# Output projection of a two-layer hybrid block: six of eight block pairs by seven products, the gated terms added to x in DRAM

## What is computed

```python
D_MODEL = 2048
D_FF = 4 * D_MODEL
...
    # gated merge of the D_MODEL-wide branch projections, then one output projection
    br = jnp.stack([o_att, o_fnet, o_ssm.astype(o_att.dtype), o_gmlp], axis=2)  # (b,L,4,MIX_W)
    gates = jax.nn.sigmoid(gate_logits.reshape(b, L, N_BRANCH, D_MODEL))
    merged = jnp.sum(gates * jnp.einsum('blkw,kwd->blkd', br, w_branch), axis=2)
    x = x + g1 * (merged @ w_out)
    # channel mixer: squared-ReLU MLP
    h2 = _rms(x) * (1 + sc2) + sh2
    x = x + g2 * (jnp.square(jax.nn.relu(h2 @ w_ff1)) @ w_ff2)
```

## Time and profile before

| | us |
|---|---|
| three timed runs | 4756.03, 4796.99, 5115.18 |
| median | 4796.99 |
| the profiled execution | 4768.78 |
| its span on the slowest core (core 1) | 4767.3 |
| spans of the eight cores | 4731.1 to 4767.3 |
| PE busy | 4562.7 (96% of the span) |
| DVE, ACT, POOL busy | 2463.3, 1910.8, 914.6 |
| output projection in the span, layer 0 and layer 1 | from 1336.6 and from 3633.6, some 137 each |

### The profile page before, as it was taken

The page is one execution under the profiler, slowest core; times in us unless marked ns, Lnnn a source line. Parts: engine busy times, 40 slices in busy tenths (PEclk is TensorE's granted clock), DMA queues, the critical chain, the costliest instruction groups (busy, mean ns, idle before and its releaser), DMA issues.

```text
span 4767.3 us, 90058 instructions; the slowest of 8 cores (4731.1 to 4767.3 us)
## 1 busy us (share of the span) xinstructions
PE 4562.7 (96%) x31548; PEld 2878.4 (60%) x31548; DVE 2463.3 (52%) x5081; ACT 1910.8 (40%) x4031; POOL 914.6 (19%) x1362
## 2 busy tenths in 40 slices
PE   3989898999999999999999998999999999999999
PEld 1445455566655777777755544655666567777776
DVE  4266645565546444444564575555654644444343
ACT  2134523333225444353544453333322453535352
POOL 1122110000101232424112201000010014141404
PEclk9979999999999999999999999999999999999999
DMA  8862755446776797979778446334578459494949
GB/s 192 136 118 65 170 99 99 80 85 128 131 198 122 120 152 121 152 118 154 159 191 150 92 109 124 67 63 79 109 136 196 100 95 148 76 151 74 153 72 128
DMA packets 266571, 585.63 MB, mean 123 GB/s; under 512 B 43792, under 2 KB 137488, under 8 KB 265872
## 3 DMA queue, kind: packets, MB, share of 16 engines
q0 software_dynamic: 171072, 441.53, 57.4%
q1 hardware_dynamic: 95056, 138.34, 9.1%
HBM read 818.05 MB, written 129.76 MB: 199 GB/s over the span
## 4 chain that ended last, share of the span: by engine, by line
PE 89%; DMA 6%; issue 2%; DVE 2%; ACT 1%; POOL 0%; SPq 0%; DVEq 0%; ACTq 0%; POOLq 0%
PE psum L1837 38%; PE psum L692 20%; PE psum L1651 18%; PE psum L1616 5%; DMA arena<-wm 2%; PE psum L1092 1%; DMA mgs<-arena 1%; PE psum L833 1%; PE psum L1074 1%; DMA arena<-wg 1%; PE psum L1133 1%; ACT arena L743 1%; DMA arena<-lc 1%; PE psum L1094 1%; DVE arena L754 1%
## 5 line engine op out<-in xcount | busy, mean ns | idle before, releaser
L1837 PE MATMUL psum<-arena 128*128 128x320 f16 x13216 | 1802.8, 299 | 0.0
L1837 PEld LDWEIGHTS psum<-arena 128*128 128x128 f16 x13216 | 1289.5, 98 | 508.7 <-issue 10.1
L754 DVE TENSOR_TENSOR arena<-arena 128x1024 f16<-128x1024 f16 (+9 forms) x2178 | 1080.6, 519 | 662.6 <-PE psum L1837 334.9
L743 ACT ACTIVATE arena<-arena 128x320 f16<-128x320 f32 (+8 forms) x1687 | 825.3, 508 | 870.1 <-DVE arena L754 528.3
L692 PE MATMUL psum<-arena 128*128 128x512 f16 (+2 forms) x5680 | 1092.0, 352 | 16.7 <-DVE arena L758 8.4
L1651 PE MATMUL psum<-arena 128*128 128x320 f16 x6720 | 1009.3, 300 | 14.7 <-ACT arena L743 6.0
L692 PEld LDWEIGHTS psum<-arena 128*128 128x128 f16 x5680 | 556.1, 99 | 504.1 <-issue 98.8
L754 DVE TENSOR_TENSOR arena<-psum,arena 128x320 f32<-128x320 f32 (+5 forms) x1110 | 539.2, 490 | 617.5 <-PE psum L1651 239.9
L1651 PEld LDWEIGHTS psum<-arena 128*128 128x128 f16 x6720 | 637.5, 98 | 330.9 <-issue 92.4
L743 ACT ACTIVATE arena<-psum,arena 128x320 f32<-128x320 f32 (+3 forms) x904 | 487.1, 554 | 664.7 <-PE psum L1837 531.8
L769 ACT COPY arena<-psum 128x320 f32<-128x320 f32 (+6 forms) x683 | 293.5, 440 | 581.8 <-PE psum L1837 259.4
(11 more groups left out here) (107 smaller groups left out, 1455.5 us busy)
## 6 DMA issues: line engine op xcount, KB each, us to landing
arena<-w POOLq DMA_DIRECT2D x256, 512.0 KB, 7.0
arena<-wm POOLq DMA_DIRECT2D x192, 512.0 KB, 7.4
arena<-wg POOLq DMA_DIRECT2D x128, 512.0 KB, 6.2
y<-arena POOLq DMA_DIRECT2D x256, 160.0 KB, 7.3
xs<-arena POOLq DMA_DIRECT2D x192, 160.0 KB, 8.2
arena<-xin SPq DMA_DIRECT2D x32, 640.0 KB, 23.5
arena<-xs SPq DMA_DIRECT2D x32, 640.0 KB, 14.9
arena<-dftA SPq DMA_DIRECT2D x32, 512.0 KB, 4.4
```

The lines of the kernel that those rows point to most:

```text
L743: return e.activation(out=lz(o), in_=lz(i), func=func, scale=scale, **kw)
L754: lambda e: e.tensor_tensor(out=lz(o), in0=lz(a), in1=lz(b), op=op), r=r, w=w, prio=S.p - boost, tag=tag)
L1837: ins = e.matmul(ps.ap()[:, 0:SUBS], lhsT=wv(kc), rhs=rhs(kc), start=first and kc == 0, stop=kc == 7, skip_group_check=True)
```

## The change

- Pairs (5,13), (4,12), (3,11), (2,10), (1,9), (0,8) of the output projection go through `sunits` with their own weight sums (`wsums`, which writes one of the four sums over a weight block, leaving one buffer of `SL` for the squares). Blocks 6, 14, 15 and 7 stay dense, as one group of four, last.
- The input sums of `M` (`tsums`) are made at the end of the gates, into `hT`, which the gates' last products still read.
- The gated quadrants go into seven buffers `XW` (the last pair partly into `hT`) and are added to x in DRAM: to `xs` in layer 0, to `y` in layer 1. So x has to be there first: in layer 0 twelve rows are copied from `xin` to `xs` inside DRAM (SP queue, during the Fourier projection); the last product of layer 0 now stores x to `y`.
- After each pair its two rows are loaded back (SP queue, after the adds have landed), squared and added up in buffers of their own (`unit_squares`).
- The planner's cost of an `addto` goes from 8 to 4 bytes an element. The tanh buffers of `gates_end` move.

Blank and unchanged lines are left out of the diff, and so are the removed copies of `cuts`, `gscale`, `gadd` and `gstore` (they are the same functions, now in `gated_terms`).

```diff
@@ -1553,6 +1553,7 @@
+        THE = [A(140 + 0.625 * i, [320]) for i in range(8)]
@@ -1616,7 +1617,7 @@
-                        th = TH[gui[1] % 8]
+                        th = (TH if bc == "B" else THE)[gui[1] % 8]
@@ -1758,7 +1759,7 @@
-            S.dma("pool", dst[fc][:, t0:t0 + n], src, 128 * n * 8, r=[src], w=xkeys(fc, t0, n), tag="xadd", accum_op=ALU.add)
+            S.dma("pool", dst[fc][:, t0:t0 + n], src, 128 * n * 4, r=[src], w=xkeys(fc, t0, n), tag="xadd", accum_op=ALU.add)
@@ -1773,6 +1774,23 @@
+        wslot = [[0, 1, 2]]
+        def wsums(ra, rb, p):
+            o1_, o2_, o4_ = wslot[0]
+            sl = [o2_, o1_, o4_]
+            wslot[0] = sl
+            s1, s2, s4 = (SL[i] for i in sl)
+            q = lambda r, h: (lambda: r.ap(F16)[:, 1024 * h:1024 * h + 1024])
+            keep_ = S.p
+            S.p = p
+            tt("dve", s1, q(rb, 0), q(rb, 1), ALU.add, 1024, [rb], [s1], x=2)
+            tt("dve", s2, s1, q(ra, 0), ALU.subtract, 1024, [ra, s1], [s2], x=2)
+            tt("dve", q(rb, 0), q(ra, 0), q(rb, 0), ALU.subtract, 1024, [ra, rb], [rb], x=2)
+            tt("dve", s4, q(ra, 1), s2, ALU.subtract, 1024, [ra, s2], [s4], x=2)
+            S.p = keep_
+            return s1, s2, None, s4
@@ -1792,7 +1810,8 @@
-        def sunits(units, act, Ts, epi, gated=None, tag="st"):
+        def sunits(units, act, Ts, epi, gated=None, tag="st", mk=None, hook=None):
+            mk = mk or ssums
@@ -1803,7 +1822,7 @@
-            sums[0] = ssums(*raws[0], S.p - 10)
+            sums[0] = mk(*raws[0], S.p - 10)
@@ -1815,7 +1834,7 @@
-                         ("P", k8(s3), s3, 2, False), ("P", w8(rb, 1), rb, 3, False), ("R", k8(s4), s4, "B22", False))
+                         ("P", w8(rb, 0) if s3 is None else k8(s3), rb if s3 is None else s3, 2, False), ("P", w8(rb, 1), rb, 3, False), ("R", k8(s4), s4, "B22", False))
@@ -1840,7 +1859,7 @@
-                            gscale, gadd, gstore = gated
+                            gscale, gadd, gstore, XT = gated
@@ -1851,8 +1870,9 @@
-                                gscale(XSt[s_ * 4 + 2], ps, bb, c1)
-                                gstore(bb, c1, XSt[s_ * 4 + 2])
+                                x3 = XT(s_ * 4 + 2)
+                                gscale(x3, ps, bb, c1)
+                                gstore(bb, c1, x3)
@@ -1874,7 +1894,57 @@
-                    sums[u + 1] = ssums(*raws[u + 1], S.p - 10)
+                    sums[u + 1] = mk(*raws[u + 1], S.p - 10)
+                if hook is not None:
+                    hook(ba, bb, u == n - 1)
+        def cuts(c):
+            return [(0, SUBS, 0)] if c < 960 else [(0, 64, 0), (64, SUBS, 1)]
+        def gated_terms(l, jg, dst, XT):
+            col = lambda blk, s: modT[l][:, s, jg + blk:jg + blk + 1]
+            def gscale(o, ps, blk, c):
+                for (u, v, s) in cuts(c):
+                    act_op(o[:, u:v], (lambda u=u, v=v: ps.ap()[:, u:v]), AF.Identity, v - u, [ps], [o[:, u:v]], scale=col(blk, s), boost=BOOST)
+            def gadd(slot, b, ps, blk, c):
+                x = XT(slot)
+                for (u, v, s) in cuts(c):
+                    stt_(x[:, u:v], (lambda u=u, v=v: ps.ap()[:, u:v]), col(blk, s), b[:, u:v], ALU.mult, ALU.add, v - u, [ps, b[:, u:v]], [x[:, u:v]], ps=True, boost=BOOST)
+                return x
+            def gstore(blk, c, x):
+                addto(blk, c, SUBS, x, dst)
+            return gscale, gadd, gstore, XT
+        WT = [hT[:, 0:8, 640:1280], hT[:, 0:8, 0:640], hT[:, 8:16, 0:640], hT[:, 8:16, 640:1280]]
+        XW = [A(kb + 1.25 * i, [320], F32) for kb, m in ((145, 4), (106, 3)) for i in range(m)]
+        xwi = [0]
+        PRA = A(105, [512])
+        TMXF = TMX.rearrange("p a b -> p (a b)")
+        SQA = [(0, 512, SL[3].bitcast(F32)), (512, 768, TMXF[:, 0:256]), (768, 1024, TMXF[:, 256:512]), (1024, 1280, A(ov + 5.125, [256], F32))]
+        sqn = [0]
+        def unit_squares(fc, first, lastunit, lastrow):
+            x = X[fc]
+            keep_ = S.p
+            S.p = keep_ + (-60 if lastunit else 4)
+            for i, (a, b, av) in enumerate(SQA):
+                m = b - a
+                if first:
+                    act_op(av, x[:, a:b], AF.Square, m, [x[:, a:b]], [av])
+                    continue
+                if lastunit:
+                    sqi[0] = (sqi[0] + 1) % 4
+                    t = hT[:, 8 + sqi[0], 512:512 + m].bitcast(BF16)
+                else:
+                    sqn[0] ^= 1
+                    t = (PRA[:, 0:m] if m == 512 else PRA[:, 256 * sqn[0]:256 * sqn[0] + m]).bitcast(BF16)
+                act_op(t, x[:, a:b], AF.Square, m, [x[:, a:b]], [t])
+                o = accs(a, b)[0][2] if lastrow else av
+                tt("dve", o, av, t, ALU.add, m, [av, t], [o])
+            S.p = keep_
@@ -1908,7 +1978,12 @@
+            nf = len(S.ops)
+            if l == 0:
+                pf = [o.id for o in S.ops[nf:] if o.eng == "pe"]
+                for i, fc in enumerate((5, 13, 4, 12, 3, 11, 2, 10, 1, 9, 0, 8)):
+                    S.dma("sp", xs[fc], xin[fc], 128 * T * 8, w=xkeys(fc, 0, T), prio=S.p + 100, tag="xcp").preds.add(pf[i * len(pf) // 12])
@@ -1921,25 +1996,44 @@
-            order = [13, 14, 15] + list(range(2, 13)) + [0, 1]
+            pG = S.p
+            for i in range(8):
+                S.p = pG - GU * (7 - i) + 4
+                tsums(M, WT, i)
+            S.p = pG
+            tail = [6, 14, 15, 7]
+            rd = y_o if last else xs
+            src = xin if l == 0 else rd
-            reload_x(order, xin if l == 0 else xs, l > 0)
+            reload_x(tail[:2], src, l > 0)
-            seen = set()
+            started = []
+            def after_unit(ba, bb, final):
+                for fc in (ba, bb):
+                    load(X[fc], rd[fc], 128 * T * 4, r=xkeys(fc, 0, T), tag="xld")
+                    unit_squares(fc, not started, final, final and fc == bb)
+                    started.append(fc)
+            def xt(i):
+                if len(started) == 10:
+                    return XW[4 + i // 4] if i % 4 == 0 else hT[:, i - 1 - i // 4, 0:640].bitcast(F32)
+                xwi[0] += 1
+                return XW[xwi[0] % 7]
+            sunits([(i, i + 8, wo[l, i], wo[l, i + 8]) for i in (5, 4, 3, 2, 1, 0)], M, WT, None, gated=gated_terms(l, 32, rd, xt), tag="swo", mk=wsums, hook=after_unit)
+            reload_x(tail[2:], src, l > 0)
-                sq_acc(blk, t0, n, tgi not in seen)
-                seen.add(tgi)
+                sq_acc(blk, t0, n, False)
-                if blk == order[-1]:
+                if blk == tail[-1]:
-                if blk == order[-1] and tgi == 1:
+                if blk == tail[-1] and tgi == 1:
-            dense([(b, wo[l, b]) for b in order[:11]], M, ev, tag="wout", ko=ko)
-            dense([(b, wo[l, b]) for b in order[11:]], M, ev, group=5, tag="wout", ko=ko)
+            dense([(b, wo[l, b]) for b in tail], M, ev, group=4, tag="wout", ko=ko)
@@ -1961,9 +2055,6 @@
...
@@ -1974,18 +2065,7 @@
...
+            gated2 = gated_terms(l, 80, y_o if last else xs, lambda i: XSt[i])
@@ -1993,7 +2073,7 @@
-                spill(blk, t0, n, X[blk][:, t0:t0 + n])
+                spill(blk, t0, n, X[blk][:, t0:t0 + n], y_o)
@@ -2022,7 +2102,7 @@
-                    sunits([pair2(i) for i in range(8)], M, ATs, None, gated=(gscale, gadd, gstore), tag="sf2")
+                    sunits([pair2(i) for i in range(8)], M, ATs, None, gated=gated2, tag="sf2")```

TensorE, end of the gates in layer 0, before: L1651 and L1616 are the gates' products, L692 the output projection.

```order
L1651 MATMUL psum<-arena 128x320 x8
L1616 MATMUL psum<-arena 128x320 x4
L1651 MATMUL psum<-arena 128x320 x4
L692 MATMUL psum<-arena 128x512 x4
L1616 MATMUL psum<-arena 128x320 x4
L692 MATMUL psum<-arena 128x512 x4
L1616 MATMUL psum<-arena 128x320 x4
L692 MATMUL psum<-arena 128x512 x24
```

13 lines of the change are left out of this document (1 added, 12 removed).

## The result

The changed kernel takes 4831.7 us in the profiled execution, 4860.2 and 4879.1 in two others, against 4768.8 before: ratio **1.018, 95% interval 1.010 to 1.027**. Repeated beside the experiments it gave 1.0135 (1.009 to 1.018). The forecast was 4778, the range 4738 to 4830, "same" 0.95; the three executions lie 2, 30 and 49 us above the range. The direction of the sum (+9) was right, its size was not: +63 us between the two profiled executions, which are what the rest of this text accounts for.

The account below looks back on a forecast made before the run. The prediction took TensorE (PE) as the bound, without gaps in the projection. Matmuls saved, pairs' start, DMA waits and copies gave - 25.6 + 4 + 30 + 1 = +9.4 on 4768.8, so 4778 us, range 4738 to 4830.

Parts of the forecast that it names:

- PE, saved: In the output projection, six pairs by seven products save 12.8 us of matmuls a layer, 25.6 in both, all on the path.
- Start of the pairs: Behind the gates, PE waits for DVE's input sums of the last gated row: 2 us a layer, 4 in all.
- input sums: Sums for the other rows, made by DVE during the gates, cost nothing, 1 us a layer at most.
- DVE and ACT at nothing: In the pairs, some 10 and 9 us of DVE and ACT work hide behind 14.93 us of PE: no cost.
- DMA: In the pairs, 19.1 us of transfers in 14.93 of PE; waits cost 15 us a layer (4.5 to 25), 30 in all.
- row 7's: PE's wait for row 7 of x, queued behind a load awaiting the last add: 4.5 us even if nothing is queued.
- The norm at nothing: Behind the projection, the norm's tiles come late but row 7's wait covers them: nothing more, up to 5 us a layer.
- Copies, 1 us: Copying twelve rows inside DRAM in layer 0, with the DFT matrices queued behind, costs 1 us, bounds 0 and 8.
- The sign that the prediction had named: New PE gaps in layer 0's Fourier stage, listed among what would show the forecast wrong.
- Rival 3: In the pairs, the add, load, square loop with loads landing after the median 14.7 us: 34 us a layer, 4834 us; chance 0.19.
- Rival 2: The add, load, square loop sets the pairs' pace, nearly every load at its maximum of 23.2 us: 4919 us; chance 0.04.
- The rule of the Trainium skill: HBM limit of some 358 GB/s per core: a pair's 6.0 MB takes an estimated 16.8 us, some 10 us of backlog.

Follow-up runs that it names:

- resident_six: The changed kernel with x of its six pairs kept in SBUF, no DRAM adds, reloads or copies; 4753.1 us, 0.9968 of the kernel before.
- run 9: Same run as resident_six: the changed kernel with x of its six pairs kept in SBUF; 4753.1 us, 0.9968 of the kernel before.
- before_again: The kernel before, unedited, profiled again on its neighbours' chip; from the gates' end through the MLP's first dense part 195.4 / 192.9 us (layers 0 / 1).
- free_load: The changed kernel with twelve rows reloaded from the kernel's input, waiting for no add; gates' end through MLP's first dense part 197.4 / 184.4 us, change 225.1 / 208.6.
- three_pairs: The changed kernel with three pairs instead of six, ten blocks dense; gates' end through MLP's first dense part 202.7 / 197.7 us, change 225.1 / 208.6.
- run 8: The kernel before with only the twelve DRAM copies added; PE gap in layer 0's Fourier stage 5.9 us in the mean, none in the kernel before.
- run 3: The changed kernel with rows reloaded from the kernel's input, without waiting (stage 197.4 / 184.4 us) or only after each pair's last matmul (219.8 / 201.3).

## Why the prediction was wrong, step by step

- **PE, saved, 12.8 us a layer: right.** The gapless stage of resident_six is 17.5 us shorter than before, of which about 5 is the shift named above.
- **Start of the pairs, 2 us a layer: wrong.** The longest wait for a DVE sum there is 0.2 us. But the stretches ahead of the stage are 1.7 and 0.4 us longer than before beyond the shift (1.8 and 1.9 in the repeats); run 9, which has neither adds nor copies, shows the same and more (3 to 4 us over before_again, less the shift). So it is neither of those. What is left is the input sums, put at "1 us at most", or the new order; not told apart.
- **DVE and ACT at nothing: right**, and by run 9 with even more DVE work.
- **DMA.** The demand was right: 19.1 us a pair, six pairs 115 us; core 1 shows a share of 1.06 over the 112 us to 1447, 119 us. The add's price was 1.14, measured 1.2 to 1.26. The waits that the term named, pairs and row 7, were put at 15 us a layer and are 18.0 in layer 0 and 17.0 in layer 1 in the mean (17.5 and 20.9 on core 1), between the chosen value and the upper bound of 25. Their parts were not as argued: row 7's, at least 4.5 "even if nothing is queued", is 2.8 and 4.2 in the mean (0 to 7.5 on the cores), so that bound was none, and the rest is in the pairs.
- **The norm at nothing, weights behind it not named: the first step that failed.** "Its tiles come late, but behind row 7's wait, which covers them" - it does not: 8.6 us at the norm, and 5.7 for weights of the MLP, in layer 0, and 2.4 at the norm in layer 1 (7.4, 5.2 and 3 on core 1). In free_load, three_pairs and resident_six, where the last rows come in time, PE has no wait for ACT there (core 1). A weight wait of 3 to 4 us in layer 0 stays in these three, so the weights have a cause of their own, which stays open.
- **The clock: the step that was missing.** Every gap was priced as idle time alone. PE ran slower in the stages with gaps, 14 us a layer, 28 in both (24 in the repeat): about the whole gain. That the gaps bring it rests on where the slow stretches lie and on run 9, without gaps at full clock; no run varies the clock alone, and the two cores of layer 1 with 30 us of it had the fewest gaps.
- **Copies, 1 us: wrong**: 4 to 5 us by the gap named in run 8, within its bounds of 0 and 8. The sign that the prediction had named, PE gaps in the Fourier stage of layer 0 that weren't there, came true.

Sum with the measured terms: - 25.6 + 52 (idle, 33.0 + 19.5 less 0.5) + 28 (clock) + 2 (input sums or order) + 4 (copies) = 60; measured 62 in the mean of the cores' spans (4807.9 less 4745.8), 63 on the slowest. Some 2 us more are clock that resident_six, the yardstick, lost itself in layer 0.

Rival 3 had the number (4834) by luck. It asked for 34 us a layer in the pairs, where 15.2 and 12.5 were lost, and had neither norm nor clock. Its loop is there in the chain, but with the loop cut and the traffic left, only 5 to 7 us a layer come back (run 3). Its own condition, a load landing after 14.7 us, was not met (9.8). Rival 2's figure for a landing of 9.75 us, 3.4 us a pair or 14 a layer, is close to what the pairs lost, but run 3 shows that most of it stays lost without the loop. The rule of the Trainium skill that the prediction weighed (DMA: Bandwidth & Descriptors, "Where 436 GB/s comes from"), a limit by bytes, does not decide here: run 9 moves more bytes in the same time without a stall.

## What to carry to other kernels

That one stage runs at a DMA share of 1.05 without a stall says little of the next. Here, at 1.08, the rows loaded back and the buffers of `XW` stood behind the adds, and their landing time became PE's; which difference between the two stages decides was not tested by itself. An ACT or DVE named as releaser is to be followed back one step: where cutting one ring of waits changes nothing, another of the same length takes over, and the cause is the resource that both share. Price a row of gaps twice: as idle time, and by the clock that may be lost with them. And measure a side effect where it happens: the copies looked free in a stretch that began 160 us behind them.

## Of the hardware, not expected

- An accumulating DMA of 160 KB takes an estimated 1.2 to 1.26 us of the 16 engines, a plain one 0.49, and it comes in packets under 2 KB: 6854 of them with the change, 1184 with plain stores.
- Idle time and clock trade: in layer 1 of the change cores 6 and 7 had only 12.9 and 9.3 us idle but a clock of 0.85 and 0.84, and a stage of 216 us; the other six, 20 to 24 us idle at 0.95 or 0.96, took 205 to 208. Why these two fell lower isn't shown, and in the repeat no core did (0.94 to 0.98).
